# Output squares of a pair of tiles added on VectorE, their sum by one product; gate weights' parts side by side; p loaded feature-major

## What is computed

```python
# first block
u = rmsnorm(h, g_mix_pre); proj = u @ w_in            # q, k, v of 8 "moba" heads, 4 "diff" heads of width 256, two gates
oa = causal softmax attention, 8 heads of 128
ob = rmsnorm(softmax(q1 k1) v - lam * softmax(q2 k2) v, sub_g) * (1 - lambda_init)   # 4 heads of 256
mixed = sigmoid(ga) * (oa @ w_br_moba) + sigmoid(gb) * (ob @ w_br_diff)
h = h + rmsnorm(mixed @ w_out, g_mix_post)
h = h + rmsnorm(relu(rmsnorm(h) @ w_up) ** 2 @ w_down, g_mlp_post)
h = h + rmsnorm((p @ w_ple_proj) * sigmoid(rmsnorm(h) @ w_ple_gate), g_ple_post)
# second block
z = rms_norm(x, mix_norm_g) @ w_in_2                  # 4 mlstm heads of 256, 8 "fox" heads, 16 gate columns
ha = rms_norm(mlstm(q, k, v, gates), mlstm_out_g) * sigmoid(mo)     # norm over each head's 256
hb = forgetting attention of the 8 fox heads
x = x + concat(ha, hb) @ w_out_2
x = x + (gelu(causal_dwconv(a)) * g) @ w_down_2
x = x + sigmoid(rms_norm(x) @ w_ple_gate_2) * (p_2 @ w_ple_proj_2)
```

## Time and profile before

| | us |
|---|---|
| median of 3 runs | 2799.41 |
| lowest, highest | 2799.23, 2799.84 |
| the profiled execution, its own time | 2799.03 |
| its span | 2797.3 |
| TensorE busy | 2762.0 |
| VectorE busy | 1782.3 |
| ScalarE busy | 1381.5 |

### The profile page before, as it was taken

One profiled execution on the slowest core, in us unless ns is written; L12 is line 12 of the kernel. 1 busy time (PEld: TensorE's weight loads), 2 busy tenths in 40 slices (PEclk: granted clock), 3 DMA queues, 4 the chain that ended last, 5 costly groups with the idle time before them and its releaser, 6 DMA issues.

```text
span 2797.3 us, 39735 instructions
## 1 busy us (share of the span) xinstructions
PE 2762.0 (99%) x14588; PEld 2358.7 (84%) x14588; DVE 1782.3 (64%) x2172; ACT 1381.5 (49%) x1815; POOL 36.8 (1%) x43
## 2 busy tenths in 40 slices
PE   8999999999999999999999999999999999999999
PEld 6888888888888888888877888888888888888887
DVE  7676766665655656556566666665676567657655
ACT  4555554455544434444466555554544344434453
POOL 2000000000000000000000000000000000000000
PEclk9999999999999999999999999999999999999999
DMA  7555546565556556556656555545555555555653
GB/s 265 177 180 166 176 158 197 193 189 182 188 196 194 189 191 190 192 184 197 208 166 207 181 165 180 166 157 185 183 182 195 195 180 182 204 185 182 233 185 136
DMA packets 413226, 521.97 MB, mean 187 GB/s; under 512 B 8544, under 2 KB 320048, under 8 KB 412496
## 3 DMA queue, kind: packets, MB, share of 16 engines
q1 hardware_dynamic: 410384, 510.64, 55.6%
q0 software_dynamic: 2752, 10.11, 1.2%
HBM read 516.51 MB, written 4.21 MB: 186 GB/s over the span
## 4 chain that ended last, share of the span: by engine, by line
PE 94%; DVE 3%; ACT 2%; issue 1%; DMA 0%; SPq 0%; ACTq 0%; DVEq 0%
PE ps L1943 39%; PE ps L1945 19%; PE ps L1953 11%; PE ps L1955 11%; PE ps L1954 11%; PE pw L2061 1%; DVE split L1139 1%; PE pw L2008 0%; DVE X L1252 0%; ACT split L563 0%; PE pw L2062 0%; ACT junk L602 0%; PE pw L2056 0%; PE pw L2050 0%; ACT cross L569 0%
## 5 line engine op out<-in xcount | busy, mean ns | idle before, releaser
L1139 DVE TENSOR_TENSOR split<-raw,split 128x1024 fp32r<-128x1024 f32 x960 | 1156.9, 1224 | 690.9 <-ACT split L563 686.0
L563 ACT ACTIVATE split<-raw 128x1024 fp32r<-128x1024 f32 x960 | 1003.0, 1055 | 812.6 <-PE ps L1955 446.6
L1943 PE MATMUL ps<-X,split 128*128 128x512 f32 x4096 | 1294.4, 397 | 13.4 <-DVE split L1139 9.3
L1945 PEld LDWEIGHTS ps<-X,split 128*128 128x128 f32 x4096 | 770.3, 188 | 182.1
L1945 PE MATMUL ps<-X,split 128*128 128x256 f32 x4096 | 805.7, 278 | 0.0
L1943 PEld LDWEIGHTS ps<-X,split 128*128 128x128 f32 x4096 | 626.6, 189 | 17.1 <-issue 11.0
L1953 PE MATMUL ps<-split,X 128*128 128x512 f32 x1408 | 550.3, 391 | 4.6 <-ACT E L779 1.2
L1955 PE MATMUL ps<-split,X 128*128 128x512 f32 x1408 | 548.1, 389 | 0.0
L1954 PE MATMUL ps<-split,X 128*128 128x512 f32 x1408 | 547.9, 389 | 0.0
L1953 PEld LDWEIGHTS ps<-split,X 128*128 128x128 f32 x1408 | 264.4, 188 | 60.8 <-DVE split L1139 1.9
L1955 PEld LDWEIGHTS ps<-split,X 128*128 128x128 f32 x1408 | 264.3, 188 | 55.1
(11 more groups left out here) (239 smaller groups left out, 1124.2 us busy)
## 6 DMA issues: line engine op xcount, KB each, us to landing
raw<-in_w_up SPq DMA_DIRECT2D x152, 1024.0 KB, 5.5
raw<-in_w_in SPq DMA_DIRECT2D x134, 1024.0 KB, 5.2
raw<-in_w_down SPq DMA_DIRECT2D x108, 1024.0 KB, 5.1
raw<-in_w_out SPq DMA_DIRECT2D x32, 1024.0 KB, 5.1
raw<-in_w_ple_gate SPq DMA_DIRECT2D x32, 1024.0 KB, 5.1
raw<-in_w_br_moba SPq DMA_DIRECT2D x8, 1024.0 KB, 5.5
raw<-in_w_br_diff SPq DMA_DIRECT2D x8, 1024.0 KB, 5.1
raw<-in_w_ple_proj SPq DMA_DIRECT2D x4, 1024.0 KB, 5.1
```

Source lines behind the costliest of these rows:

```text
L563: A(split[:, k % RING, :, 0, :], raw[:, (k // 2) % RING, HALF * (k % 2):HALF * (k % 2) + HALF, :], ACT.Copy).then_inc(hi_done, 1)
L1139: TT(split[:, k % RING, :, 1, :], raw[:, (k // 2) % RING, HALF * (k % 2):HALF * (k % 2) + HALF, :], split[:, k % RING, :, 0, :], ALU.subtr ...
L1943: MM(ps[:, 2 * s + j, :], stay[:, 0, j * P:j * P + P], move, start=start, stop=False, skip_group_check=True)
L1945: ins = MM(ps[:, 2 * s + j, 0:TOK], stay[:, 1, j * P:j * P + P], move[:, 0, :], start=False, stop=stop, skip_group_check=True)
```

## The change

Four edits:

- VectorE adds the two tiles of squares (`o_pair_sum`) in the first half of the next head, behind that half's `lo`, and `sum_o` is one product of the sum.
- `sum_o` and the finish steps go from half 2 to half 3; in the branch stage TensorE's wait for `o_ready` 12 goes from half 4 to half 5.
- The gate product has the 32 columns of both parts as its stationary side: one 512-wide product for each k-tile, into 32 partitions. ScalarE copies all of it, and VectorE brings partitions 16 to 31 down with a shuffle and adds three quarters instead of two halves.
- p and p_2 are handed to the kernel feature-major, loaded so, and split by ScalarE and VectorE from where they land. The transposes go.

```diff
@@ -501,7 +501,7 @@
         pool.wait_ge(o_ready, 12)
-        pool.dma_start(emb[0], a["p"][0, 0].rearrange("(a p) d -> p a d", p=P)).then_inc(p_landed, 16)
+        pool.dma_start(emb[0], a["p_t"].rearrange("p (f t) -> p f t", f=2)).then_inc(p_landed, 16)
         pool.wait_ge(gated, 8)
@@ -515,7 +515,7 @@
         pool.wait_ge(hid_ready, 32)
-        pool.dma_start(emb[1], a["p_2"][0, 0].rearrange("(a p) d -> p a d", p=P)).then_inc(p_landed, 16)
+        pool.dma_start(emb[1], a["p_2_t"].rearrange("p (f t) -> p f t", f=2)).then_inc(p_landed, 16)
         for j in range(6, 12):
@@ -704,7 +704,7 @@
                     gate_a(s, i + 4)
-                if m == 2 and not isinstance(i, int):
+                if m == 3 and not isinstance(i, int):
                     finish_diff(i - 1)
@@ -719,7 +719,7 @@
             def after(m):
-                if isinstance(i, int) and i == 0 and m == 2:
+                if isinstance(i, int) and i == 0 and m == 3:
                     finish_diff(3)
@@ -750,8 +750,8 @@
         def embed(k, operand):
-            act.wait_ge(p_turned, k + 1)
-            A(operand[:, :, 0, :], pw[:, 2, :].rearrange("p (a t) -> p a t", a=2), ACT.Copy).then_inc(p_hi, 1)
+            act.wait_ge(p_landed, 16 * (k + 1))
+            A(operand[:, :, 0, :], emb[k], ACT.Copy).then_inc(p_hi, 1)
         def out1(i):
@@ -945,7 +945,7 @@
                 act.wait_ge(ple_left, 16 * 4)
-                gate_step(2, GR[0:16, 0], pw[0:16, 0, TOK:512], ACT.Copy)
+                gate_step(2, GR[0:32, 0:2], pw[0:32, 0, :].rearrange("p (a t) -> p a t", a=2), ACT.Copy)
                 gate_step(5, GR[0:16, 2], GR[0:16, 1], ACT.Abs)
@@ -965,7 +965,7 @@
                     gate_steps(m)
-                elif m == 2:
+                elif m == 3:
                     finish_mlstm(i - 1)
@@ -1026,7 +1026,7 @@
                     softmax_exps(18 + 4 * i)
-                if i == 0 and m == 2:
+                if i == 0 and m == 3:
                     finish_mlstm(3)
@@ -1324,6 +1324,10 @@
                 TT(X2[:, bass.ds(tile + hh, 1), 1, :], pw[:, 2 + hh, 0:TOK].unsqueeze(1), X2[:, bass.ds(tile + hh, 1), 0, :], ALU.subtract).then_inc(o_ready, 1)
+        def o_pair_sum(n):
+            dve.wait_ge(o_squares, n + 1)
+            TT(MX[:, 2, :], MX[:, 2, :], MX[:, 3, :], ALU.add).then_inc(o_pair_sums, 1)
+
         def o_inverse_root(n):
@@ -1399,7 +1403,9 @@
                     evac_normed(s, 3, t[:, (s.u + 3) % 2], mix_rn)
-                if m == 2 and not isinstance(i, int):
+                if m == 0 and not isinstance(i, int):
+                    o_pair_sum(i - 1)
+                if m == 3 and not isinstance(i, int):
                     finish_diff(i - 1)
@@ -1417,7 +1423,9 @@
             def after(m):
-                if isinstance(i, int) and i == 0 and m == 2:
+                if isinstance(i, int) and i == 0 and m == 0:
+                    o_pair_sum(3)
+                if isinstance(i, int) and i == 0 and m == 3:
                     finish_diff(3)
@@ -1452,7 +1460,7 @@
             dve.wait_ge(p_hi, k + 1)
-            TT(operand[:, :, 1, :], pw[:, 2, :].rearrange("p (a t) -> p a t", a=2), operand[:, :, 0, :], ALU.subtract).then_inc(p_ready, 1)
+            TT(operand[:, :, 1, :], emb[k], operand[:, :, 0, :], ALU.subtract).then_inc(p_ready, 1)
         def out1(i):
@@ -1649,7 +1657,10 @@
                 dve.wait_ge(gates, 2)
-                TT(GR[0:16, 1], pw[0:16, 0, 0:TOK], GR[0:16, 0], ALU.add).then_inc(gates, 1)
+                steps.step(nc.vector.stream_shuffle(GR[0:32, 2], GR[0:32, 0], HALVES_SWAPPED))
+                steps.step(TT(GR[0:16, 1], GR[0:16, 0], GR[0:16, 1], ALU.add))
+                settled()
+                TT(GR[0:16, 1], GR[0:16, 1], GR[0:16, 2], ALU.add).then_inc(gates, 1)
                 dve.wait_ge(gates, 3)
@@ -1686,7 +1697,9 @@
             def after(m):
-                if m == 2 and not first:
+                if m == 0 and not first:
+                    o_pair_sum(i + 3)
+                if m == 3 and not first:
                     finish_mlstm(i - 1)
@@ -1768,6 +1781,10 @@
                 q = 2 * i + r
+                if i == 0 and m == 0:
+                    o_pair_sum(7)
+                if i == 0 and m == 3:
+                    finish_mlstm(3)
                 if m % 12 == 3:
@@ -1789,8 +1806,6 @@
                     o_lo_heads(16 + 4 * i, 8 + 4 * i)
-                if i == 0 and m == 2:
-                    finish_mlstm(3)
                 if i == 1 and m == 3:
@@ -2074,9 +2089,8 @@
         def sum_o(n):
-            pe.wait_ge(o_squares, n + 1)
-            MM(pw[:, 1, 0:TOK], ones, MX[:, 2, :], start=True, stop=False)
-            MM(pw[:, 1, 0:TOK], ones, MX[:, 3, :], start=False, stop=True).then_inc(o_sums, 1)
+            pe.wait_ge(o_pair_sums, n + 1)
+            MM(pw[:, 1, 0:TOK], ones, MX[:, 2, :], start=True, stop=True).then_inc(o_sums, 1)
         def moba(i):
@@ -2113,35 +2127,22 @@
                     weigh_tiles()
-                if m == 2 and not isinstance(i, int):
+                if m == 3 and not isinstance(i, int):
                     sum_o(i - 1)
         def finish_diff(m):
-            if m == 2:
+            if m == 3:
                 sum_o(3)
-            if m == 4:
+            if m == 5:
                 pe.wait_ge(o_ready, 12)
         loop(pe, Chain(None), 4, 0, lambda i: each_half(At("branch", i, 8, 6), BRANCH), start=1)
-        def embed(k):
-
-            pe.wait_ge(p_landed, 16 * (k + 1))
-            for f in range(2):
-                for q in range(2):
-                    ins = T(pw[:, 2, f * TOK + q * P:f * TOK + q * P + P], emb[k][:, q, f * P:f * P + P], ident)
-            ins.then_inc(p_turned, 1)
-
         def out1(i):
-            s = At("out1", i, 8, 2)
-
-            def before(m):
-                if i == 0 and m == 2:
-                    embed(0)
-            each_half(s, OUT1, x1_is(1), before)
+            each_half(At("out1", i, 8, 2), OUT1, x1_is(1))
         out1(0)
@@ -2221,7 +2222,7 @@
         each_half(at, GATE, x1_is(3), last_turn, start=4)
-        each_half(At("gate1", 1, 8, 2), GATE, x1_is(3), lambda m: embed(1) if m == 2 else None)
+        each_half(At("gate1", 1, 8, 2), GATE, x1_is(3))
         s = At("proj2")
@@ -2240,8 +2241,7 @@
                 for kt in range(KT):
-                    MM(pw[0:16, 0, :], gate_split[:, kt, 0, :], X1[:, kt], start=kt == 0, stop=False, skip_group_check=True)
-                    ins = MM(pw[0:16, 0, 0:TOK], gate_split[:, kt, 1, :], X1[:, kt, 0, :], start=False, stop=kt == KT - 1, skip_group_check=True)
+                    ins = MM(pw[0:32, 0, :], gate_split[:, kt].rearrange("p a c -> p (a c)"), X1[:, kt], start=kt == 0, stop=kt == KT - 1)
                 ins.then_inc(gates, 1)
@@ -2405,6 +2405,8 @@
     arrays["columns"] = np.concatenate([np.asarray(inputs[name]).reshape(n, P).T for name, n in VECTORS], 1)
+    for name in ("p", "p_2"):
+        arrays[name + "_t"] = np.ascontiguousarray(arrays.pop(name)[0, 0].T.reshape(2, P, TOK).transpose(1, 0, 2)).reshape(P, 2 * TOK)
     arrays["constants"] = CONSTANTS
```

More of the change, by code:

```diff
@@ L267, in two_blocks @@
     x_turned, eps_ready, zeros_ready = sem("x_turned"), sem("eps_ready"), sem("zeros_ready")
-    p_turned, p_hi, p_ready = sem("p_turned"), sem("p_hi"), sem("p_ready")
+    p_hi, p_ready = sem("p_hi"), sem("p_ready")
     lam_parts, lam_summed, lam_exps = (sem(n) for n in ("lam_parts", "lam_summed", "lam_exps"))
@@ L277, in two_blocks @@
     probs_turned, pt_ready, pv_done = sem("probs_turned"), sem("pt_ready"), sem("pv_done")
-    o_raw, o_squares, o_sums, o_root, o_normed, o_hi, o_ready = (sem(n) for n in ("o_raw", "o_squares", "o_sums", "o_root", "o_normed", "o_hi", "o_ready"))
+    o_raw, o_squares, o_pair_sums, o_sums, o_root, o_normed, o_hi, o_ready = (sem(n) for n in ("o_raw", "o_squares", "o_pair_sums", "o_sums", "o_root", "o_normed", "o_hi", "o_ready"))
     sig_done, gated, ple_gated, out_ready = (sem(n) for n in ("sig_done", "gated", "ple_gated", "out_ready"))
```

## The result

| | before | after |
|---|---|---|
| median, us | 2799.23 (5 runs) | 2814.60 (5 runs) |
| lowest, highest | 2798.55, 2799.84 | 2813.36, 2816.41 |
| ratio | | 1.0055, 95% interval 1.0043 to 1.0066 |
| profiled execution, its span | 2799.03, 2797.3 | 2815.16, 2813.4 |

The changed kernel is 15.4 us slower, 0.55%. The forecast was 12.1 us, 2811.5, in a range of 2805.5 to 2815. The median lies 0.4 inside that range; two of the five runs, the profiled one among them, lie above it.

The account below looks back on a forecast made before the run. TensorE bounds the kernel, busy 2762.0 of 2797.3 us. Terms -5.16 + 12.6 (mlstm) + 1.7 (fox) + 2.86 (branch) + 0.15 (diff) = +12.1 us on 2799.4 give 2811.5, range 2805.5 to 2815.

Parts of the forecast that it names:

- The gains: Work taken from TensorE: sum_o products -3.40 us, gate product -0.87, transposes of embed -0.89; sum -5.16 us.
- the lead: Three halves by which hi and lo run ahead, 8.36 us; diff heads' chain takes 8.35, so +0.15 us in all.
- The term of 2.35 us: Mlstm heads 1 to 3: loss at the start of half 7, chain 10.71 us against 8.36.
- fox and branch: Later finish costs +1.7 us in fox's half 3 and +2.86 at the branch stage's half 5.
- R2: Clock falls after the branch stage's wait, 2.1 us lost: +14.2, 2813.6 us; chance 0.15.
- the second wait: Mlstm heads 1 to 3, before the scores at half 9: unit 1 evacuated late, 1.84 us lost per head.
- The mlstm terms: Losses at half 7 and before the scores: 4.19 us per head, +12.6 for three heads.
- missed sign: TensorE's busy time should fall by about 6 us and its idle time rise by about 18.
- R1: No wait before the mlstm scores, only half 7 is late: +6.6, 2806.0 us; chance 0.10.
- R3: Not slower: finish steps fit in the lead, added waits vanish: 2794.2 us, or 2797 with branch wait; chance 0.07.
- R4: Edits to the gates and to p do nothing measurable: +13.9, 2813.3 us; chance 0.05.
- The rule on table loads: A drain of some 1.38 us per ScalarE table switch would lengthen the chains, total near +27 us; not in the trace.

Follow-up runs that it names:

- move only: Kernel before with only sum_o and the finish steps moved to half 3 and the o_ready wait to half 5: 2818.5 us, ratio 1.0068.
- late exponentials: Changed kernel with ScalarE's exponentials of mlstm heads 1 to 3 in half 7, behind unit 1's evacuation, not half 5: 2811.78 us, ratio 1.0039.
- Sqrt first: Changed kernel with ScalarE's finish step ahead of unit 0's evacuation in half 3 of mlstm heads 1 to 3, fox and branch: 2799.72 us, ratio 1.0001.
- pair early: Kernel of move undone with the pair addition moved from the next head's half 0 to the head's own end: 2795.93 us, ratio 0.9987.
- move undone: Changed kernel with sum_o and the finish steps back in half 2, o_ready wait back at half 4: 2800.35 us, ratio 1.0005.
- o_ready at half 6: Kernel of pair early with the branch stage's wait for o_ready 12 at half 6, not half 4: 2793.22 us, ratio 0.9977.
- gates alone: Kernel before with the gate edit alone: 2798.79 us, ratio 0.9998.

## Why the prediction was right, point by point

**The gains.** Diff heads are 0.35 us shorter each (forecast 0.375: 0.425 for the product, less 0.05 for the lead that is just used up). p gave 0.5 at gate1 in the profile, forecast 0.45. The gates came 0.9 earlier, forecast 0.87; the shuffle took 0.43, a little over its upper bound of 0.41, and the product with 32 columns kept the pace but for its start-up: 16 of them take 3.89 us, 1535.18 to the next start at 1539.07, where the 32 products of before took 5.80, so 1.91 went for the 1.87 forecast.

**mlstm.** The waits stand where they were put, but for that before head 1's scores. At half 7 the idle time is 1.9 where 2.2 was said, at the scores 1.6 for 1.7 in heads 2 and 3. The term of 2.35 us is about 2.15 (0.91 of idle cost 1.17 in the branch stage of before, so 1.9 costs 2.15), because 0.81 from L1338 to the next instruction was taken over from before, where a `lo` stood behind it; it is 0.61. The head's period grew by 3.6 us (48.7 to 52.3), forecast 4.19 less 0.425.

**fox and branch.** 1.45 idle for the 1.6 said, and 3.78 for the 3.9.

**Rival R2, the clock, happened**, at full cost in the branch stage: that stage's stretch grew by 4.6 us, and the terms without the clock give 2.86 - 0.425 - 0.44 = 2.0. The remaining 2.6 is near the 2.1 worked out from the earlier trace rows. What the prediction didn't name is that the same could happen behind waits of 1.7 and 1.9 us. It did at the gates (1.5 us), and in mlstm head 1, where the second wait swallowed it. The mlstm terms came out some 0.6 us lower, the clock took 4.1; with 0.5 at the start this is the step from 12.1 to the profiled 16.1.

The falls also account for most of the missed sign. TensorE counts as busy while it works at half its clock, and the three falls add 2.6, 1.5 and, in half 7 of head 1, 1.5 us of busy time. The idle time lacks what head 1 would have waited before its scores, and 0.95 at the start, which isn't edited (7.79 after 8.74).

**What was luck.** The mechanism and its terms held, but the time is that of the forecast with R2, to which the prediction gave 0.15 against 0.63 for the forecast itself, which is 3.1 us under the median. The range had room for one fall, not for two: the median is inside because the mlstm terms came out lower, and by only 0.4 us.

The forecast of 2811.5 is about the time with the clock up at the two places where a fall costs something: with TensorE kept busy through these waits the same changed kernel takes 2810.4.

**Rivals R1, R3 and R4** fell: the scores came 7.4 us after the start of half 7 in every head, the lead was too short by about what was said, and the gates and p earned their part. The rule on table loads was rightly set aside: the Trainium skill, "ScalarE: Activation LUTs", What ACT_TABLE_LOAD costs, would put a drain of some 1.4 us beside each load, and here the Sqrt starts at 1592.54, 1.29 after the load's start at 1591.25. The clock fell behind the wait of 3.78 us and, in some executions, behind those of 1.66 and 1.9. The Trainium skill, "TensorE: Matmul & The Clock Gate", Why this matters for your kernels, warns of gaps between bursts of matmuls that bring half rate back; with this the trace agrees at 3.78 us, and here gaps shorter than those it warns of did it too.

## What to carry to other kernels

When a step is moved later in an engine's program, look at what it now stands behind, not at how far it went: one half later left 1.0 us of wait in each of three heads, behind an instruction that waits for the end of that half it cost 15 us more. Then count what is queued behind the moved step, up to the second and third customer. And when an added instruction is late for its reader, look for the engine's idle gap ahead of it before moving the reader: the pair addition, put into VectorE's gap at the head's end, together with a wait placed at its first real need, turned a loss of 0.55% into a gain of 0.23%.

## What the runs showed of the hardware

- A wait far shorter than that of the start (8.74 us before) can take TensorE's clock down to 1.2 GHz. Behind 3.8 us of idle it fell in all three profiles with that wait (changed, move only, late exponentials); behind 1.66 us at the gates it fell in four of seven profiles with that wait (changed, Sqrt first, late exponentials, pair early) and stayed up in three (move undone, o_ready at half 6, gates alone); behind 1.9 us in mlstm it fell six times of twelve, in one or two heads of three in each of four profiles. Behind waits of 0.9 to 1.58 us it stayed up in all profiles. A fall cost 1.5 us, and 2.6 in the one place where TensorE was slow from its first product on.
- Plain fp32 products of constants in the wait kept it up: 1.00 from 424 to 432 us, over the filler in the branch stage and behind it, where the changed kernel has 0.50 behind the wait.
- A fall costs nothing where TensorE would soon have waited for something else: mlstm periods of 52.33 us with one and 52.30 without.
